# Conditioning matmuls of a decoder trunk: four column sets of one row tile in four strips, turned by a block transpose

## What is computed

```python
def ada_modulate(c, w, b):
    m = jax.nn.silu(c) @ w + b          # w is 2048 x 6144
    shift, scale, gate = jnp.split(m[:, None, :], 3, axis=-1)
    return shift, scale, gate

def modulated_norm(x, g, shift, scale):
    return rmsnorm(x, g) * (1.0 + scale) + shift
...
        x = x + gate * y                # y: the mixer's output
        shift, scale, gate = ada_modulate(c, W["ada_mlp_w"][layer], W["ada_mlp_b"][layer])
        h = modulated_norm(x, W["norm_mlp"][layer], shift, scale)
        x = x + gate * sq_relu_mlp(h, W["mlp_w1"][layer], W["mlp_w2"][layer])
```

## Time and profile before

| | us |
|---|---|
| median of three runs | 3193.6 |
| profiled execution, whole | 3191.07 |
| its span (first to last instruction) | 3189.3 |
| TensorE busy | 3101.5 |
| VectorE busy | 1476.2 |
| ScalarE busy | 1105.6 |
| GpSimd busy | 29.6 |

### The profile page before, as it was taken

One profiled execution on the slowest core, in us unless ns is written; L12 is line 12 of the kernel. 1 busy time (PEld: TensorE's weight loads), 2 busy tenths in 40 slices (PEclk: granted clock), 3 DMA queues, 4 the chain that ended last, 5 costly groups with the idle time before them and its releaser, 6 DMA issues.

```text
span 3189.3 us, 54574 instructions
## 1 busy us (share of the span) xinstructions
PE 3101.5 (97%) x21299; PEld 2845.2 (89%) x21299; DVE 1476.2 (46%) x2075; ACT 1105.6 (35%) x1345; POOL 29.6 (1%) x55
## 2 busy tenths in 40 slices
PE   8999998999999999999999999999899999999998
PEld 4888854598899889889889899999899999999998
DVE  3556544356334334334335545555544444444443
ACT  3334343234332333333332433333433333333332
POOL 0000000100000000000000000000000000000000
PEclk9999998999999999999999999999999999999999
DMA  9987789745765774775775344444344444444443
GB/s 329 336 272 230 238 321 347 275 140 166 252 216 167 256 235 160 239 243 163 231 240 182 126 148 148 151 148 150 121 151 149 147 151 147 149 151 147 149 151 105
DMA packets 507991, 624.37 MB, mean 196 GB/s; under 512 B 17728, under 2 KB 403521, under 8 KB 507524
## 3 DMA queue, kind: packets, MB, share of 16 engines
q1 hardware_dynamic: 499840, 595.66, 57.4%
q0 software_dynamic: 6112, 22.84, 1.9%
q10 hardware_dynamic: 1926, 4.24, 0.4%
HBM read 617.13 MB, written 5.54 MB: 195 GB/s over the span
## 4 chain that ended last, share of the span: by engine, by line
PE 93%; DVE 2%; DMA 2%; issue 2%; ACT 1%; POOL 0%; POOLq 0%; SPq 0%; ACTq 0%; DVEq 0%
PE mm L1652 86%; PE aux L1652 6%; DMA wide_later<-in_ada_mlp_w 1%; PE mm L1785 1%; DMA wide_first<-in_ada_mix_w 1%; DVE tmp L1046 0%; DMA kpage<-in_cache_k 0%; DVE h_lo L1072 0%; PE aux L2009 0%; DVE tmp L1062 0%; DVE tmp L1065 0%; DVE p_s L1458 0%; DVE w_lo L978 0%; ACT ares L588 0%; DVE p_s L1480 0%
## 5 line engine op out<-in xcount | busy, mean ns | idle before, releaser
L978 DVE TENSOR_TENSOR w_lo<-raw,w_hi 128x1024 fp32r<-128x1024 f32 x752 | 919.5, 1225 | 1345.8 <-ACT w_hi L571 1344.3
L571 ACT ACTIVATE w_hi<-raw 128x1024 fp32r<-128x1024 f32 x752 | 795.0, 1058 | 1704.9 <-PE mm L1652 1704.9
L1652 PE MATMUL mm<-h_hi,w_hi 128*128 128x320 f32 x3712 | 1168.7, 315 | 25.7 <-DVE h_lo L1072 18.2
L1652 PE MATMUL mm<-h_hi,w_lo 128*128 128x320 f32 x3712 | 1152.3, 310 | 0.0
L1652 PE MATMUL mm<-h_lo,w_hi 128*128 128x320 f32 x3712 | 1152.0, 310 | 0.0
L1652 PEld LDWEIGHTS mm<-h_hi,w_hi 128*128 128x128 f32 x3712 | 701.6, 189 | 125.4 <-issue 93.6
L1652 PE MATMUL mm<-u_hi,w_hi 128*128 128x320 f32 x2304 | 714.0, 310 | 0.0
L1652 PE MATMUL mm<-u_hi,w_lo 128*128 128x320 f32 x2304 | 711.9, 309 | 0.0
L1652 PE MATMUL mm<-u_lo,w_hi 128*128 128x320 f32 x2304 | 711.9, 309 | 0.0
L1652 PEld LDWEIGHTS mm<-h_lo,w_hi 128*128 128x128 f32 x3712 | 702.4, 189 | 0.1
L1652 PEld LDWEIGHTS mm<-h_hi,w_lo 128*128 128x128 f32 x3712 | 701.7, 189 | 0.0
(11 more groups left out here) (273 smaller groups left out, 1140.0 us busy)
## 6 DMA issues: line engine op xcount, KB each, us to landing
raw<-in_mlp_w SPq DMA_DIRECT2D x512, 512.0 KB, 3.6
narrow<-in_ada_mlp_w SPq DMA_DIRECT2D x64, 1024.0 KB, 5.2
raw<-in_w_in_odd SPq DMA_DIRECT2D x96, 512.0 KB, 3.6
raw<-in_w_in_even SPq DMA_DIRECT2D x80, 512.0 KB, 6.7
narrow<-in_ada_mix_w SPq DMA_DIRECT2D x40, 1024.0 KB, 5.2
wide_later<-in_ada_mlp_w SPq DMA_DIRECT2D x64, 512.0 KB, 8.7
wide_first<-in_ada_mix_w SPq DMA_DIRECT2D x58, 512.0 KB, 8.5
raw<-in_w_out_even SPq DMA_DIRECT2D x32, 512.0 KB, 3.4
```

Of the source, the lines that this page charges most:

```text
L571: fn(w_hi[:, slot], raw[:, slot], ACT.Copy).then_inc(hi_ready, 1)
L978: v.tensor_tensor(w_lo[:, slot], raw[:, slot], w_hi[:, slot].bitcast(F32), ALU.subtract).then_inc(lo_ready, 1)
L1652: return nc.tensor.matmul(out, lhsT, rhs, start=first, stop=last)
```

## The change

In 36 of the 48 groups (all but those of the first mixer) the unit becomes a part: 2048 columns, three for each matrix, nine in all. A load is one row tile of 128 rows by 2048 columns, rows of 8 KB where they were 2 KB; 1 MB in `narrow` as before, and 1 MB in each of four wide slots in place of eight of 512 KB. `part_tile` sends the same K-tile to all four strips: strip n gets the columns 128t + 32n + i for t in 0..15 and i in 0..31, read as 16 runs of 32. Each strip adds up over all 16 K-tiles, so nothing is left to be summed over strips. One transpose on VectorE turns each 32x32 block of the bank straight from PSUM into `ares`, after which partition 32n + i holds its nine values of column tile t at 32t; one multiply-add with the bias writes 16 tiles of `mod`. For these parts ScalarE's copies, TensorE's folds and the small bias additions go, and TensorE waits for `ada_turned` before it begins the next part in the bank. In the MLP the four inward turns of a block hold one part in `acc`; the gate part of the third matrix is gathered over the four blocks, four K-tiles in each, in a second bank, `acc_gate`, and turned in the last block. On TensorE the blocks and turns of this MLP are written out; only the six plain outward pairs remain a loop.

```diff
-WIDE = 8
+WIDE = 4
...
-        wide_later = at("wide_later", RW, [P, WIDE, 2, GCOLS])
+        wide_later = at("wide_later", RW, [P, WIDE, D])
...
+        acc_gate = mm[:, 2, 1, :]
...
+        narrow_row = narrow.rearrange("p k n -> p (k n)")
...
+        def ada_rows(W, row, part):
+
+            return W[bass.ds(row, P), bass.ds(part * D, D)]
...
-        MOD_READY = [8, 24, 48, 48]
+        MOD_READY = [8, 15, 21, 21]
...
+            def ada_wide(a, part):
+
+                for n in range(KT):
+                    slot = KW.now % WIDE
+                    if KW.now >= WIDE:
                         sp.wait_ge(wide_used, KW.now - (WIDE - 1))
...
+                    sp.dma_start(wide_later[:, slot], ada_rows(ADA[a], P * n, part)).then_inc(wide_in[slot], 16)
                     KW.up()
...
+                for n in range(4):
+                    sp.wait_ge(narrow_used, KN.now)
+                    sp.dma_start(narrow_row, ada_rows(ADA[a], row + P * n, part)).then_inc(narrow_in, 16)
+                    KN.up()
+                    for src in sources[2 * n:2 * n + 2]:
+                        load(src)
...
-                if i % 4 == 3:
-                    ada_out(True)
...
-                    if h % 2 == 0:
-                        ada_out(True)
...
+            def ada_part(a, part, bank, *done):
+
+                dve.wait_ge(*done)
+                dve.wait_ge(mod_ready, AG.now)
+                AG.up()
+                AT.up()
+                v.transpose(ares[:, :], bank).then_inc(ada_turned, 1)
+                dve.wait_ge(ada_turned, AT.now)
+                bias = vec[:, bass.ds(part * KT + ADA_B[a], KT)].unsqueeze(2).broadcast_to([P, KT, NC])
+                v.scalar_tensor_tensor(mod[:, a, bass.ds(part * KT, KT), :],
+                                       ares.rearrange("p (t c) -> p t c", c=32)[:, :, 0:NC], 0.5, bias, ALU.mult, ALU.add
+                                       ).then_inc(mod_ready, 1)
...
+                    if part is not None:
+                        NU.up(16)
+                        ada_part(*part, acc, narrow_used, NU.now)
+                        NU.up(4)
...
-            ada_bias(1, 3)
+            ada_part(1, 0, acc, narrow_used, 24)
...
+                if h == 0:
+                    ada_part(1, 1, acc, wide_used, KT)
...
+                if b == 0:
+                    ada_part(1, 2, acc, wide_used, 2 * KT)
...
-            ada_bias(2, NB // 2 - 1)
+            ada_part(2, 0, acc, wide_used, 3 * KT)
...
+            def part_tile(bank, k, row):
+
+                cols = row.rearrange("p (t s i) -> p s t i", s=4, i=32)
+                for n in range(4):
+                    strip = slice(32 * n, 32 * n + 32)
+                    ins = mul(bank[strip, :].rearrange("p (t i) -> p t i", i=32), cs[:, k, :], cols[:, n], k == 0, k == KT - 1)
+                return ins
+
+            def ada_wide():
+
+                slot, k = KW.now % WIDE, KW.now % KT
+                if k == 0:
+                    pe.wait_ge(ada_turned, KW.now // KT + 1)
+                pe.wait_ge(wide_in[slot], 16 * (KW.now // WIDE + 1))
+                part_tile(acc, k, wide_later[:, slot]).then_inc(wide_used, 1)
+                KW.up()
+
+            def ada_part(bank, k):
+
+                pe.wait_ge(narrow_in, KN.now * 16 + 16)
+                part_tile(bank, k, narrow_row).then_inc(narrow_used, 1)
+                KN.up()
...
-                    ada(range(2 * (i % 4), 2 * (i % 4) + 2))
+                    ada_wide()
...
-                if i < 16 and i % 4 == 3:
-                    fold()
...
-                ada(range(4 * r, 4 * r + 2))
+                ada_wide()
...
+            def mlp_with_parts(count):
+
+                for b in range(BLOCKS):
+                    pe.wait_ge(ada_turned, b + 4)
+                    turn_with_part(h_hi, h_lo, acc, 0, h_inputs(count),
+                                   ((pair_free, G.now + 1), lambda: (pair_free, G.now + 2)), R)
+                    for i in range(1, 4):
+                        turn_with_part(h_hi, h_lo, acc, 4 * i, None,
+                                       ((relu_out, R.now - 1), lambda: (relu_out, R.now - 1)), R)
+                    relu = R.now
+                    turn_with_part(u_hi, u_lo, acc_gate, 4 * b, u_block(),
+                                   ((relu_out, relu - 1), lambda: (relu_out, relu)))
                     with looped(pe, 1, 4, {K: 8, G: 2}):
                         for r in range(2):
                             pair(r, u_hi, u_lo)
```

More of the change, by code:

```diff
@@ L404, in turn_with_ada, with turn_with_part @@
                         load(src)
+            def turn_with_part(src1, a, part, row, after):
+                sources = [src1(s) for s in range(SLOTS)]
+                if after is not None:
+                    sources += [after(s) for s in range(SLOTS)]
+                for n in range(4):
[4 more added lines that the diff above has]
+                        load(src)
             def matrix(W, pairs, first=0):
@@ L707, in rounds, with mlp @@
                     split()
[L709 to L716, removed]
+            def mlp(last):
                 def hidden(r, j, ahead=4):
@@ L725, in block_ @@
                 def block_(ahead):
[L726 to L746, removed]
+                    with looped(act, 0, 4, {K: 8, U: 2}) as i:
+                        split()
+                        hidden(0, i * 4)
+                        split()
+                        hidden(1, i * 4 + 2)
+                    rounds(7 + ahead)
+                with looped(act, 0, BLOCKS - last, {K: 64, U: 8}):
                     block_(1)
@@ L924, in _ @@
             norm()
-            mlp(0, 5)
+            mlp(0)
             root()
@@ L1298, in hidden, with block_ @@
                                     ALU.subtract).then_inc(u_ready, 1)
[L1300 to L1310, removed]
+                def block_(ahead, part=None, squares=False, gate=False):
+                    with looped(dve, 0, 4, {K: 8, R: 2, U: 2}) as i:
+                        split()
+                        hidden(0, i * 4)
+                        split()
+                        hidden(1, i * 4 + 2)
+                    if part is not None:
+                        NU.up(16)
+                        ada_part(*part, acc, narrow_used, NU.now)
+                        NU.up(4)
                     if ahead:
-                        outward(n, squares, second)
+                        outward(n, squares, (lambda: ada_part(2, 2, acc_gate, narrow_used, NU.now)) if gate else None)
                     else:
@@ L1733, in fold, with turn_with_part, burst @@
                 ins.then_inc(fold_done, 1)
+            def turn_with_part(hi, lo, bank, first, inputs=None, free=(None, None), count=G, after=None):
+                def burst(first):
+                    return lambda s: ada_part(bank, first + s // 2) if s % 2 == 0 else None
+                pair(0, hi, lo, inputs, free[0], count, before=burst(first))
+                pair(1, hi, lo, None, free[1]() if free[1] else None, count, before=burst(first + 2), between=after)
             def turn_with_ada(hi, lo, inputs=None, free=(None, None), count=G, after=None):
@@ L2012, in _ @@
                 ins.then_inc(s_o, 1)
-                ada(chunks[3:4])
-            fold()
-            pe.wait_ge(mod_ready, F.now)
             pe.wait_ge(s_norm, 1)
@@ new lines, in u_block @@
+            def u_block():
+                base, off = UB.base, UB.off
+                UB.up(8)
+                return lambda s, kk: pe.wait_ge(u_ready, base + (off + 2 * s + 2)) if kk == 0 else None
+            def mlp_with_parts(count):
[9 more added lines that the diff above has]
+                                   ((relu_out, relu - 1), lambda: (relu_out, relu)))
+                    with looped(pe, 1, 4, {K: 8, G: 2}):
+                        for r in range(2):
+                            pair(r, u_hi, u_lo)
```

178 lines of the change are left out of this document (71 added, 107 removed).

## The result

The changed kernel takes 3167.4 us (median of 4 runs, 3164.8 to 3169.3) against 3192.9 for the kernel before, run on the same chip (4 runs, 3185.8 to 3196.1): a ratio of 0.9925, 95% interval 0.9910 to 0.9939. It is faster by 25.5 us, where the sum forecast 39.0 us (3155 us). 3167.4 lies inside the range that was given, 3141 to 3180, and in that of rival A, but 12 us above the forecast and outside its own narrow range of 3150 to 3160.

A forecast was written before the change was run, and what follows sets the result against it. TensorE was taken to bound the kernel, except in attention, where transfers and a chain of short steps set the pace. 3.6 + 17.8 + 5.6 + 12 = 39.0 us gave 3155 us, range 3141 to 3180.

The forecast's parts named there:

- rival A: Attention stage: transfers keep it as long as it is, gain there 0 to 7 us; 3160 to 3172 us, chance 0.25.
- The fold at 0.89 us: Input projection and first MLP: each removed TensorE fold of strips saves 0.89 us, 3.6 us and 17.8 us.
- Bursts at no cost: Conditioning bursts on TensorE: same matmuls and columns, operand in runs of 32 columns at step 128, priced at 0.
- Rival C: Bursts: moving operand breaks the strips' overlap, 0.94 us more each, 3290 us; chance 0.08, plus 0.08 for a part.
- The jumps back in layer 0: First MLP's block loop on TensorE: three issue waits at jumps back go when written out, 5.6 us.
- What unrolling takes away: First MLP written out on TensorE: 5.6 us of issue waits go; longer straight code priced at 0.
- Attention, 12 us forecast: Attention stage: gain of 12 us taken between chain and transfer caps, bounds -2 and +17.
- a chain of 17: Attention stage: removed folds and copies save 18.9 us, less 2 us for transposes: 17 if nothing else bound.
- a cap by rate of 10 to 22: Attention transfers, 69.3 MB: gain capped at 10 us at 391 GB/s, 22 with 8 KB rows at 430 GB/s.
- the text's own sign: First part of attention, GB/s at share 1.05: 387 speaks for transfers holding the stage, over 410 for rival B.
- rival B: Attention: long rows move at 430 GB/s and the chain gets its 17 us; 3150 down to 3143 us, chance 0.14.
- The transposes: VectorE: nine transposes of about 0.7 us; 0 on the MLP's path, 2 us charged in attention.

## Why the prediction was right or wrong, step by step

- **The fold at 0.89 us: right.** A block lasts 249.01 us, forecast 249, and the input projection gave 3.3 us of 3.6 from the span's start, 3.5 by its own length. The way to the number held: a difference of two rows of one chain, 8.12 and 7.23, with and without the thing that is removed.
- **Bursts at no cost: right.** 0.99 and 1.00 us with runs of 32 columns at a step of 128. Rival C, chance 0.16 with its partial form, had only the spread between two bounds for it; the equal rows of 245 and 246 ns were the better guide.
- **The jumps back in layer 0: right, 5.6 us,** and the written-out blocks have no gap. The MLP of layer 0 gave 22.4 of 23.4.
- **"What unrolling takes away": a step that failed.** It priced the longer code by the stage in which it stands and allowed at most that the 5.6 us be lost. It did not ask what stands behind it in the program: the same body as a loop, in layer 1. Its move cost 11.2 us (5.9 standing, 5.2 at a lower clock), 10.9 by the spans, where the whole gain is 21.7. The trace of before held a hint that I passed over: the loop of layer 0 paused at each jump, and that of layer 1, the same work without the conditioning, never did. Of two such loops only one pauses, so something other than the jump decides, and the size or place of the code was the thing to ask about.
- **Attention, 12 us forecast, 6.9 found: mis-sized, and by a term that was missing.** I set the gain between a chain of 17 and a cap by rate of 10 to 22. Both hold up: the first part moves 417 GB/s in a mix (forecast 430 for 8 KB rows alone), which by the text's own sign spoke for rival B and its full 17 us, and with the keys issued early the stage does gain 17.7. But 69.3 MB divided by a rate presumes transfers that are always issued in time, and in the right order. In the changed kernel they are not: the share falls to 0.66 from 575 to 580, and TensorE waits 15.8 us for keys, which in GpSimd's queue stand behind the wait of the values' buffer, and whose landing the long rows stretch (for keys 16.1 us at most where it was 11.1, for values 22.6 where it was 11.8). The prediction charged each queue for rate, none for order. The kernel before has the same order and loses nothing by it (207.9 against 208.0 us), so its trace alone did not show the price.
- **The transposes: right, 712 ns where 688 was taken,** and the 2 us charged on attention's path are about right (2.4 us of the stage for its three transposes once more; by the medians 0.3 us, within the noise).
- **The rivals.** 3167.4 us is in rival A's range (3160 to 3172), but not for A's reason: the rate rose and the jumps were gained. Only its 0 to 7 us for attention fits. A right total for another cause is no support for the cause. That the total lies in the stated range is in part luck: the 11 us of layer 1 were in no term and under no rival.
- **The sum with both failures mended.** The kernel with layer 1 written out as well has 3157.7 us, 2.7 above the forecast of 3155, and with keys issued early 3149.9, which is rival B's 3150.

## What to carry to other kernels

Code that is added or written out moves every loop behind it: look for pauses at the turns of all later loops, read the instruction queue's packets over each, and move a loop by some dozens of instructions, or write it out, before you judge the edit. In a stage where transfers seem to set the pace, find first where they end, since a row that reaches past that point shows a low rate without a cause; then look at the load that an engine waits for, and at what stands ahead of it in its queue. Long rows raise the rate and delay other queues' loads, so both have to be priced. And where two kernels differ by a few us, compare the length of the stage that the edit concerns: here the start of the kernel alone moved by up to 6 us.

## What the runs showed of the hardware that was not expected

- The same loop on TensorE, about 1600 instructions long, runs on without a gap or pauses 1.7 to 2.3 us at each turn, and 48 or 96 instructions more in front of it decide which. With pauses, 34 packets of instructions come in during the stage, without them 6 or 7.
- The three pauses in layer 1 of the changed kernel cost 3.7 us each for 2.0 us of standing still, since the granted clock falls behind them (0.89 over the next 15 us). Not always: behind the three pauses of layer 0 in the kernel before, and behind the first pause of the kernel moved by 48 instructions, it was 1.00 over 15 us; behind that kernel's two others 0.89. What makes the difference is open.
- Rates of a single core from 425 to 515 us, by length of the wide rows: 379 to 392 GB/s for 2 KB, 410 and 411 for 4 KB, 417 for 8 KB. The Trainium skill, DMA: Bandwidth & Descriptors, section Where 436 GB/s comes from, has about 358 GB/s as the limit of HBM for a core; all of these are above it. What a second core at work would leave of them, no run here shows.
- Longer rows on one queue delay another queue's transfers: the longest landing of a 512 KB page of values goes from 12 to 15 or 16 to 22 us with rows of 2, 4 and 8 KB, at nearly the same median in the changed kernel (7.8 and 8.2 us for 2 and 8 KB), but not with the keys early (7.8, 11.7 and 14.1 us). It looks like sharing by packet instead of by byte; that was argued from these numbers and not tested by itself.
- Still open: at which boundary a loop begins to pause, whether the 3 to 6 us of 4 KB rows are real, and whether 2 KB rows cost anything once the keys are early.
